# One more weight chunk, the last head's query and key, projected beside the last expert gathers

## The reference, cut to what matters

```python
x = x + peer_ffn(rmsnorm(x, norm_ffn), ...)            # 128 expert rows per token are gathered
x = x + sigmoid(rmsnorm(x, norm_ple) @ ple_gate) * (p @ ple_proj)
...
h = _rmsnorm(x, norm_g[0, 0]) * (1.0 + scale_m) + shift_m
proj = h @ w_in                                        # 3072 columns
a_val, a_gate, q, k, v, g = jnp.split(proj, splits, axis=-1)
a = a_val * jax.nn.sigmoid(a_gate)                     # then a convolution of 31 taps
q = _rotary(q, cos, sin) * (RET_HEAD_DIM ** -0.5)      # 4 heads of 128
k = _rotary(k, cos, sin)
```

## Time and profile before

| | |
|---|---|
| median of 3 runs | 3299.95 us (3292.05, 3299.95, 3301.63) |
| the profiled execution | 3293.69 us, of which the span from first to last instruction is 3291.9 |
| mean granted TensorE clock over the span | 0.878 of full speed |
| TensorE / VectorE / ScalarE / GpSimd busy | 78% / 62% / 22% / 20% of the span |
| moved | 810.93 MB, of it 619.09 MB on GpSimd's queue |
| the expert layer, ple, the second mixer | about 520 to 1942, 1944 to 1965, 1965 to 2186 us |

### The profile page before, as it was taken

The page is one execution under the profiler, slowest core; times in us unless marked ns, Lnnn a source line. Parts: engine busy times, 40 slices in busy tenths (PEclk is TensorE's granted clock), DMA queues, the critical chain, the costliest instruction groups (busy, mean ns, idle before and its releaser), DMA issues. The chain is left out here.

```text
span 3291.9 us, 34612 instructions
## 1 busy us (share of the span) xinstructions
PE 2581.9 (78%) x13120; PEld 1490.9 (45%) x13120; DVE 2048.9 (62%) x4464; ACT 736.8 (22%) x1676; POOL 649.0 (20%) x649
## 2 busy tenths in 40 slices
PE   9999899895333453434575779999999998999998
PEld 4554545441000121101132347458844476878887
DVE  6676831777777777677776439547487686465422
ACT  2144211222111222212343221122111232211000
POOL 1211000344444444444444310000000000000000
PEclk9999999997656666657787889999999999999999
DMA  6764212799999999999999983022255563122222
GB/s 213 259 238 159 77 64 90 305 420 409 421 421 419 416 417 417 419 416 419 416 418 415 420 340 124 26 80 77 90 192 214 204 224 124 64 88 80 89 90 77
DMA packets 120567, 810.93 MB, mean 246 GB/s; under 512 B 13936, under 2 KB 16496, under 8 KB 32464
## 3 DMA queue, kind: packets, MB, share of 16 engines
q0 software_dynamic: 91312, 619.09, 46.6%
q1 hardware_dynamic: 29088, 189.62, 15.5%
HBM read 779.30 MB, written 29.36 MB: 246 GB/s over the span
## 5 line engine op out<-in xcount | busy, mean ns | idle before, releaser
L1471 PE MATMUL po<-pair,diag 128*32 128x512 f32 x1868 | 432.6, 925 | 495.4 <-ACT diag L1588 495.0
L1742 DVE SCALAR_TENSOR_TENSOR pair<-pair,shared 128x1024 f32<-128x1024 f32 x467 | 566.7, 1225 | 327.4 <-DMA pair<-in_peer_uv,idx 315.1
L1296 POOL DMA_INDIRECT pair<-in_peer_uv,idx x467 | 529.1, 1133 | 859.7 <-PE po L1471 540.8
L1471 PEld LDWEIGHTS po<-pair,diag 128*32 128x32 f32 x1868 | 77.5, 145 | 731.7 <-ACT diag L1588 581.2
L1583 ACT ACTIVATE ge<-a 128x4 f32<-128x4 f32 (+1 forms) x130 | 26.7, 205 | 949.3 <-DVE pair L1742 929.4
L1471 PE MATMUL po<-shared,diag 128*32 128x512 f32 x180 | 144.9, 953 | 109.3 <-ACT diag L1588 109.3
L2175 PE MATMUL acc<-a,ring 128*128 128x512 f32 x512 | 220.9, 592 | 0.0
L2175 PEld LDWEIGHTS acc<-a,ring 128*128 128x128 f32 x512 | 97.3, 190 | 122.0 <-issue 122.0
L1862 DVE TENSOR_TENSOR weight_sums<-ring 128x512 f32<-128x512 f32 x53 | 36.7, 692 | 167.5 <-DMA ring<-in_w_fc 151.3
L1886 PE MATMUL bank<-hT,ring 128*128 128x256 f32 x592 | 139.9, 379 | 0.0
L1886 PE MATMUL bank<-hT,weight_sums 128*128 128x256 f32 x592 | 139.8, 379 | 0.0
(11 more groups left out here) (543 smaller groups left out, 4547.7 us busy)
## 6 DMA issues: line engine op xcount, KB each, us to landing
ring<-in_w_fc SPq DMA_DIRECT2D x62, 1024.0 KB, 4.8
mg<-in_ada_w POOLq DMA_DIRECT2D x96, 512.0 KB, 5.0
tab<-s_tables SPq DMA_DIRECT2D x16, 1664.0 KB, 6.4
first<-in_w_first SPq DMA_DIRECT2D x14, 1024.0 KB, 7.1
other<-in_w_first SPq DMA_DIRECT2D x14, 1024.0 KB, 6.9
s_tables<-weight_sums POOLq DMA_DIRECT2D x8, 1664.0 KB, 6.6
s_tables<-table POOLq DMA_DIRECT2D x8, 1664.0 KB, 6.2
shared<-in_w SPq DMA_DIRECT2D x10, 1024.0 KB, 16.1
```

What stands on the lines that cost most here:

```text
L1296: pool.indirect_dma_start(out=place[at], out_offset=None, in_=core.dram["peer_uv"][:, :], in_offset=bass.IndirectOffsetOnAxis(ap=idx[:, su ...
L1471: last = pe.matmul(po[j * TOK:(j + 1) * TOK, t % 2, half * 512:(half + 1) * 512], diag[:, g % 3, i, :], place[at][:, D + half * 512:D + (h ...
L1742: dve.scalar_tensor_tensor(row, row, 1.0, h_rows[:, t % 2, j, :], ALU.mult, ALU.mult, accum_out=a[:, g % 4, i:i + 1]).then_inc(dotted, 1)
```

## The change

`SOON` was one number with two uses: how many tiles `peer` makes early (14) and, halved, how many chunks `ple` puts in place. It becomes 16, and a new number `READY = 7` takes the second use. So tiles 14 and 15 are made for 384 tokens in `peer`, after groups 127 and 128; chunk 7 is brought in for them there; it is still brought again for the mixer, into its own ring, and chunks 1 to 6 go into `core.shared` as before.

```diff
-SOON = 14
+SOON, READY = 16, 7
...
-            for c in range(1, SOON // 2):
+            for c in range(1, READY):
                 sp.dma_start(core.shared[:, 2048 * (c - 1):2048 * c], block_of(core, "w2", c)).then_inc(core.soon_landed[c - 1], 16)
...
-                if c < SOON // 2:
+                if c < READY:
...
-        core.soon_landed = [nc.alloc_semaphore(f"soon_landed_{i}") for i in range(SOON // 2 - 1)]
+        core.soon_landed = [nc.alloc_semaphore(f"soon_landed_{i}") for i in range(READY - 1)]
```

## The result

The changed kernel took 3316.55 us (median of 6 runs, 3313.12 to 3319.55) against 3300.79 us for the kernel before (median of 6, 3292.05 to 3306.36). The ratio is 1.0051, interval 1.0037 to 1.0065: slower by 15.8 us, half a per cent. The forecast was +17.6 us, to 3314.4 us, in a range of 3303 to 3323.

A forecast was written before the change was run, and what follows sets the result against it. Gathers bound the expert layer until its last groups, then TensorE; VectorE's convolution bounds the mixer. 16.1 us at the layer's end plus 1.5 in the mixer gave +17.6, on 3296.8 to 3314.4 us, range 3303 to 3323.

The forecast's parts named there:

- Two tiles ahead of the last two groups: End of expert layer: both tiles run uncovered after the last gather, 16.41 us from group 127 to `out(3)`, +11.6 us.
- Chunk 7: End of expert layer: its 1 MB transfer stretches two VectorE waits, delaying group 126 by 2.48 us; bounds 0 and 2.48.
- The slower clock at group 126: End of expert layer: after about 5.15 us idle TensorE restarts at a slower clock, +2.0 us, between 1.3 and 2.7.
- The rival without it: Expert layer's end and mixer: no slow restart at either place, sum +13.7 us; chance 0.16.
- The fetch for `ple`: Start of `ple`: weights fetched behind tile 15 still land in time, cost nothing, with 5 us to spare.
- rival 4: Start of `ple`: it waits for its weights and starts 12.7 us later, about +30 us; chance 0.03.
- The mixer: Second mixer: shorter jobs 14 and 15 put TensorE 10.1 us ahead, but it idles 8.6 us for VectorE; 0.4 us left.
- The slow clock in the mixer: Second mixer after the 8.6 us idle: slow stretch of some 5.9 us, 3.9 of it uncovered, costing 1.95 us.
- the mixer keeps its gain: Second mixer: the 10.1 us saved are kept, sum +6.0 us, no change that can be measured; chance 0.08.
- the tiles are hidden too: End of expert layer: both tiles hidden like the fourteen before, mixer keeps its gain, -10.1 us; chance 0.03.
- The stretch between: From `out(3)` through `ple` to the mixer's start: everything shifts as a whole, no cost of its own.

The follow-up runs named there:

- e3: Changed kernel without the early transfer of chunk 7, tiles 14 and 15 taking the weights lying there: 3312.88 us against 3300.23, ratio 1.0039.
- e2: Changed kernel with jobs 14 and 15 of the mixer making all 512 columns again: 3316.56 us against 3300.23, ratio 1.0051.
- e4: Kernel before with the early transfer of chunk 7 alone, used by nobody: 3304.96 us against 3300.23, ratio 1.0009.
- e6: Changed kernel with taps 15 to 30 of the first two channel groups' convolution left out: 3306.86 us, ratio to before 1.0018.
- e8: Changed kernel with tile 14 alone made early, chunk 7 still brought early: 3313.70 us against 3296.68, ratio 1.0047.
- e1: Kernel before with mixer jobs 14 and 15 making 128 columns instead of 512, nothing making the rest: 3302.60 us against 3300.23, ratio 1.0010.
- e5: Kernel before with taps 15 to 30 of the first two channel groups' convolution left out: 3299.98 us, ratio 0.9996.
- e7: Kernel before with chunk 0 of the mixer's weights fetched ahead of chunks 4 to 6 in `ple`: 3293.29 us against 3303.08, ratio 0.9974.

## Why the prediction was right

**Two tiles ahead of the last two groups, +11.6.** Measured 1955.13 - 1938.80 = 16.33 us from group 127 to `out(3)`, forecast 16.41; 11.5 more than before. e3 has the same with the transfer gone.

**Chunk 7, +2.5.** From chunk 6's issue to group 126 it is 35.42 - 33.03 = 2.4 us more in the changed kernel, 2.0 to 2.9 over e2, e4, e6 and e8, and 0 in e3. Both stretched waits fell in group 126, the one of the bounds that was taken. One reading was loose: 2.48 us for 1 MB is 423 GB/s, which is not the layer's mean of 395 but the rate at its end, 426.

**The slower clock at group 126, +2.0.** Measured 9.03 - 7.21 = 1.8; over the kernels with chunk 7 it is 1.4 to 2.9. The price is real and depends on the run, so the hit within 0.2 us is luck; that there is a price of this size is not. The rival without it (13.7 us) is told apart not by the total, in whose interval both lie (12.2 to 21.5 us, 0.0037 and 0.0065 of 3300.8), but by the granted clock and by e3 against e4.

**The fetch for `ple`, 0.** Its first matmul waits 2.90 us for `hT`, the same time as before, and not for weights. So rival 4 falls.

**The mixer, 10.1 us of TensorE's time for a gain of 0.4.** Idle 8.48 us against a forecast of 8.6. e1 shows that nothing is gained, e6 that the convolution is the cause.

**The slow clock in the mixer, +1.95.** This is the term that was too large. `turn(3)` started when VectorE let it, as forecast, but the slow stretch was over with it: 2049.68 - 2045.85 = 3.83 us for the two turns and job 18 at full speed. The stretch was 3.8 us long and not the 5.9 that were read from the mixer's start. M is 0.62 us longer and not 1.5. In e3 it reached into job 18, which took 7.53 us there and not 7.07 (M + 1.1).

**The rivals of the other sign.** That the mixer keeps its gain (+6.0), and that the tiles are hidden too (faster), fell with e1, e2 and e3.

**The stretch between, put at 0.** The prediction let `ple` and the mixer's start shift as a whole. In the changed kernel this stretch was 1.04 us shorter, of which 0.86 are the first two jobs (5.67 us, not 6.53). It was 47.25 to 50.33 us over the nine kernels without an edit there, so this is a scatter that the forecast had no term for, not an effect of the change that is shown.

From chunk 6's issue to `turn(4)` the traces give 15.74 - 1.04 + 0.62 = 15.3 us, by the measured 15.8.

**Where luck helped.** The difference was forecast 1.8 us too large, and the base of 3296.8 lay 4.0 us below the 3300.79 that was measured. The two cancel in part, and so the forecast time is only 2.1 us off. On the measured base it would have been 3318.4, inside the range all the same.

## What to carry to other kernels

Work moved into gaps is free only as long as there are gaps. Look at the brackets of the receiving engine in just those rows: here they end three groups before the stage does, and behind the last one each microsecond counts in full. Then ask of the place that is relieved who is waited for when the work is gone: an engine with no idle time may still be early, if another one's long list ends within two microseconds of it. Where both meet, take off work that stands ahead of the other's start (here the late chunk 0) and not beside it.

## What the runs showed of the hardware

The price of an idle time of 3.5 us is a coin toss. In the second mixer, untouched by all of this, TensorE waits 3.47 or 3.48 us for `conv` ahead of 24 matmul records. In five of the ten traces these took 11.99 to 12.26 us (before, e2, e3, e5, e6), in the other five 13.43 to 13.61 (changed, e1, e4, e7, e8). The row of the changed kernel:

```profile
2159.84 13.45 PE L2452 MATMUL acc<-conv,ring 128*128 128x512 f32 x24 [3.47 <-ACT conv L2566]
```

The 1.2 us between before and changed stay to the end of the stage, and are as much as some edits are tried for.

The same holds for the wait of 3.62 us at 1802.56, after which the prediction saw nothing. Its group took 1.92 us in before, changed, e3 and e6, but 2.44 to 3.64 in the six other traces, after the same 3.6 us. That row was the lucky side of a toss and no sign that such a wait is free. In e4 it reads:

```profile
1804.44 2.92 PE L1473 MATMUL po<-pair,diag 128*32 128x512 f32 x16 [3.61 <-ACT diag L1591]
```

The Trainium skill (TensorE: Matmul & The Clock Gate, Part 1: The HAM clock gate) says that the number of slow matmuls at a kernel's start varies from run to run of the same kernel. These rows agree, and show it behind idle times in the middle of a kernel: the numbers of one trace can be off by a microsecond or so at each such place.
